# Two transformer blocks on one core: first input projection by feature rows, modulation sums by pairs of feature tiles, side reads moved

## The reference, cut to what matters

```python
mod = c_act @ w_ada[l] + b_ada[l]                  # 1024 -> 3072
shift, scale, gate = jnp.split(mod, 3, axis=-1)
h = rms_norm(x, g_pre[l]) * (1.0 + scale[:, None, :]) + shift[:, None, :]
proj = h @ w_in[l]                                 # 1024 -> 3072: u_a b_a c_a gate_a u_p gate_p, 512 each
y_a = b_a * causal_depthwise_conv(c_a * u_a, w_conv[l]) * jax.nn.silu(gate_a)
y_p = causal_multiscale_pool(u_p, w_pool[l], pool_scale[l]) * jax.nn.silu(gate_p)
y = jnp.concatenate([y_a, y_p], axis=-1) @ w_out[l]
x = x + gate[:, None, :] * rms_norm(y, g_post[l])
```

## Time and profile before

| | |
|---|---|
| median of 3 runs | 1283.83 us (1282.14 to 1292.85) |
| the profiled execution | 1283.65 us, its span 1281.9 us |
| TensorE busy | 1246.6 us (97%), 7756 matmuls |
| VectorE, ScalarE, GpSimd busy | 887.8, 641.3, 171.9 us |
| mean granted TensorE clock | 0.993 of full speed |
| read from memory | 234.92 MB, mean 184 GB/s |

### The profile page before, as it was taken

The page is one execution under the profiler, slowest core; times in us unless marked ns, Lnnn a source line. Parts: engine busy times, 40 slices in busy tenths (PEclk is TensorE's granted clock), DMA queues, the critical chain, the costliest instruction groups (busy, mean ns, idle before and its releaser), DMA issues.

```text
span 1281.9 us, 19570 instructions
## 1 busy us (share of the span) xinstructions
PE 1246.6 (97%) x7756; PEld 1109.8 (87%) x7756; DVE 887.8 (69%) x931; ACT 641.3 (50%) x825; POOL 171.9 (13%) x217
## 2 busy tenths in 40 slices
PE   3899999999999999989999999999999999999998
PEld 2899899888888899978988888888889998988887
DVE  5779666676666767987766667666667787766665
ACT  2445545554444456855544444444446675644442
POOL 8400100088200120000100001000001221200000
PEclk9999899999999999999999999999999999999999
DMA  9897495455556462314555654655554444455551
GB/s 361 262 324 270 158 326 185 145 197 183 186 189 196 121 215 66 132 67 131 187 182 189 196 186 144 227 197 191 182 186 164 148 147 157 151 187 196 196 196 66
DMA packets 166816, 236.88 MB, mean 185 GB/s; under 512 B 5140, under 2 KB 146592, under 8 KB 164704
## 3 DMA queue, kind: packets, MB, share of 16 engines
q1 hardware_dynamic: 165920, 235.09, 54.9%
q0 software_dynamic: 816, 0.89, 0.3%
q10 hardware_dynamic: 16, 0.00, 0.0%
HBM read 234.92 MB, written 1.05 MB: 184 GB/s over the span
## 4 chain that ended last, share of the span: by engine, by line
PE 85%; DVE 6%; DMA 4%; ACT 2%; POOL 1%; issue 1%; DVEq 0%; ACTq 0%; POOLq 0%
PE acc L2185 23%; PE acc L2187 12%; PE acc L2221 5%; PE acc L2222 5%; PE acc L2223 5%; PE acc L2203 4%; PE acc L2204 3%; PE acc L2205 3%; DVE wlo L1349 2%; DMA raw<-in_w_ada_dram 2%; PE acc L2239 2%; PE acc L2593 2%; DMA raw<-in_w_in_dram 2%; PE acc L2241 2%; PE acc L2240 2%; PE acc L2122 2%
## 5 line engine op out<-in xcount | busy, mean ns | idle before, releaser
L1349 DVE TENSOR_TENSOR wlo<-raw,whi 128x2048 fp32r<-128x2048 f32 (+1 forms) x199 | 453.8, 2283 | 199.7 <-ACT whi L745 198.7
L745 ACT ACTIVATE whi<-raw 128x2048 fp32r<-128x2048 f32 (+1 forms) x199 | 378.1, 1904 | 184.3 <-PE acc L2223 113.1
L2185 PE MATMUL acc<-hT,whi 128*128 128x512 f32 x1280 | 320.2, 392 | 0.5 <-ACTq L826 0.5
L2185 PEld LDWEIGHTS acc<-hT,whi 128*128 128x128 f32 x1280 | 232.4, 189 | 43.9 <-issue 0.7
L2187 PEld LDWEIGHTS acc<-hT,wlo 128*128 128x128 f32 x1280 | 174.6, 190 | 12.5
L2187 PE MATMUL acc<-hT,wlo 128*128 128x256 f32 x1280 | 178.5, 282 | 0.0
L2221 PE MATMUL acc<-whi,sT_hi 128*128 128x512 f32 x320 | 125.0, 391 | 0.0
L2222 PE MATMUL acc<-wlo,sT_hi 128*128 128x512 f32 x320 | 125.0, 390 | 0.0
L2223 PE MATMUL acc<-whi,sT_lo 128*128 128x512 f32 x320 | 124.5, 389 | 0.0
L2203 PE MATMUL acc<-whi,hT 128*128 128x256 f32 x416 | 120.2, 289 | 1.1 <-DVE hT L1423 1.1
L2204 PE MATMUL acc<-wlo,hT 128*128 128x256 f32 x416 | 117.6, 283 | 0.0
(11 more groups left out here) (324 smaller groups left out, 1950.6 us busy)
## 6 DMA issues: line engine op xcount, KB each, us to landing
raw<-in_ffn_w_in_dram SPq DMA_DIRECT2D x88, 1024.0 KB, 5.1
raw<-in_ffn_w_out_dram SPq DMA_DIRECT2D x44, 1024.0 KB, 5.0
raw<-in_w_ada_dram SPq DMA_DIRECT2D x24, 1024.0 KB, 5.9
raw<-in_w_in_dram SPq DMA_DIRECT2D x24, 1024.0 KB, 5.9
raw<-in_diff_w_in_dram SPq DMA_DIRECT2D x12, 1024.0 KB, 5.2
raw<-in_nsa_w_in_dram SPq DMA_DIRECT2D x10, 1024.0 KB, 5.3
raw<-in_w_out_dram SPq DMA_DIRECT2D x8, 1024.0 KB, 4.9
raw<-in_nsa_cmp_w_dram SPq DMA_DIRECT2D x4, 1024.0 KB, 5.5
```

Of the source, the lines that this page charges most:

```text
L745: nc.scalar.activation(whi[:, w % SPL, 0:n], raw[:, r % RAW, 0:n], ACT.Copy).then_inc(hi_ready, 1)
L1349: nc.vector.tensor_tensor(wlo[:, w % SPL, 0:n], raw[:, r % RAW, 0:n], whi_f[:, w % SPL, 0:n], ALU.subtract).then_inc(raw_done, 1)
L2185: nc.tensor.matmul(o, hi[:, kt, cs], hT[:, :, kt, :], start=kt == 0, stop=False)
```

## The change

Layer 0 alone, up to its end:

- The shift and scale weights of layer 0 are read in four pairs of feature tiles. A pair is two items of 1 MB (each 4 row tiles by 256 columns of shift and 256 of scale, as two transfers). VectorE sums them in 8 `add_row` of 128 x 512, each waiting for the one before. TensorE sums over partitions (`sum_pair`), VectorE makes shift and gain of the two tiles (`pair_modulation`), ScalarE their features and `hT_hi` (`features`), VectorE `hT_lo` (`features_lo`).
- Half of `w_in` (columns 1536 to 3071) is read as 8 row items, one per feature tile (128 x 1536, 768 KB). TensorE adds each into six PSUM banks, 30 matmuls an item (`row_high`, `row_low`, `row_last`). Four of the banks are cleared with zeros first. The other half stays six column chunks (`cols1`).
- x is loaded first. The turned x is copied out of PSUM before the modulation is known. `b_ada` and `g_pre` are loaded by ScalarE's queue; GpSimd issues its parameter loads after the inverse norms. `keep_clock` shrinks from 5 calls to 1.
- The side items move: none among the rows, then two between column chunks, then one between output chunks.
- ScalarE, VectorE and TensorE have the layer's program written out by hand.

```diff
-    items = [("ada", 0, kt) for kt in range(KD)]
-    side = [("gate", 0, c) for c in range(4)] + [("ada", 1, kt) for kt in range(KD)]
-    for n, c in enumerate(IN1_ORDER):
-        items.append(("w", "in1", 0, c))
-        if n in SIDE_CHUNKS:
-            items.append(side.pop(0))
...
+    items = pair(0) + rows(0) + pair(1) + rows(1, 2) + pair(2) + rows(3, 4) + pair(3) + rows(5, 6, 7)
+    cols = [("w", "in1", 0, c) for c, _ in COLS1]
...
+    items += cols[0:2] + gate[0:2] + cols[2:3] + gate[2:4] + cols[3:4] + ada[0:2] + cols[4:5] + ada[2:4] + cols[5:6]
+    items += ada[4:6] + outs[0:1] + ada[6:7] + outs[1:2] + ada[7:8] + outs[2:4]
```

On ScalarE:

```diff
+            def features(f):
+                act.wait_ge(pair_ready, f + 1)
...
+                for k in range(2):
+                    kt = 2 * f + k
+                    step(nc.scalar.activation(h_pair[:, f % 2, k, :], xT[:, kt, :], ACT.Identity,
+                                              bias=shift1[:, 0, kt:kt + 1], scale=gain1[:, 0, kt:kt + 1]))
+                    nc.scalar.activation(hT_hi[:, kt, :], h_pair[:, f % 2, k, :], ACT.Copy).then_inc(feat_hi, 1)
...
+            split_to(0)
+            features(0)
+            split_to(1)
+            features(1)
+            split_to(2)
+            split_to(3)
+            features(2)
+            split_to(4)
+            split_to(5)
+            features(3)
```

On VectorE:

```diff
+            def add_pair(f):
+                dst = acc_pair[:, f % 2, :, :]
+                for half in range(2):
...
+                    for k in range(4):
+                        ins = add_row(dst, raw[:, r % RAW, k * 512:(k + 1) * 512].rearrange("p (s n) -> p s n", s=2),
+                                      4 * half + k)
+                        if k < 3:
+                            step(ins)
...
+            add_pair(0)
+            row_lo(1)
+            pair_modulation(0)
+            features_lo(0)
+            add_pair(1)
+            row_lo(1)
+            pair_modulation(1)
+            row_lo(1)
+            features_lo(1)
+            add_pair(2)
+            row_lo(1)
+            pair_modulation(2)
+            row_lo(1)
+            features_lo(2)
+            add_pair(3)
+            row_lo(1)
+            pair_modulation(3)
+            features_lo(3)
+            row_lo(2)
...
+                    stream_to(b0 + 4)
+                    modulation(0, 1)
+                    lambda_parts()
+                    pooled_y(0)
+                    stream_to(b0 + 5)
+                    ada_chunks(2)
```

Then `c_a * u_a` and two `y_low`, and:

```diff
+                    stream_to(b0 + 6)
+                    convolve(0)
+                    step(nc.vector.tensor_tensor(v1[:, :, :], v1[:, :, :], pf[:, 12:16, :], ALU.mult))
+                    stream_to(b0 + 7)
```

On TensorE:

```diff
+            sum_pair(0)
+            keep_clock(1)
+            row_high(0, False)
+            row_high(0, True)
+            row_low(0)
+            row_high(1, False)
+            row_high(1, True)
+            sum_pair(1)
+            row_low(1)
```

Rows 2 to 6 follow in the same way, with `sum_pair(2)` behind the first part of row 3 and `sum_pair(3)` behind the second of row 5. Then:

```diff
+            row_last(7)
...
+            cols1(0)
+            pe.wait_ge(proj_ready, 2)
+            pooled_means(0)
+            cols1(1)
+            pe.wait_ge(u_ready, TT)
+            sum_modulation(0, 1)
+            pe.wait_ge(proj_ready, 3)
+            cols1(2)
+            pe.wait_ge(proj_ready, 8)
+            mix_pooled(0)
+            cols1(3)
+            cols1(4)
+            spread_gate(0)
+            cols1(5)
```

More of the change, by code:

```diff
@@ L359, in source @@
         def source(item):
+            if item[0] == "pair":
+                f, half = item[1:]
+                return a["w_ada"][0][half * 512:(half + 1) * 512, 0:2 * D]\
+                    .rearrange("(k p) (s n) -> p k s n", p=P, s=2)[:, :, :, f * CC:(f + 1) * CC]
             if item[0] == "ada":
@@ L365, in source @@
             kind, *at = item[1:]
+            if kind == "row":
+                return a["w_in"][0][at[0] * P:(at[0] + 1) * P, ROW0:ROW0 + ROWN].rearrange("(k p) n -> p k n", p=P)
             if kind == "in1":
@@ L420, in pair_bank, with transfers @@
             return (6 if l == 0 else 2) if c == 0 else 0
+        def transfers(r):
+            return 2 if items[r][0] == "pair" else 1
         def landed_value(r, it=0):
-            return it * (16 * 6 // RAW) + 16 * (r // RAW + 1)
+            return it * (16 * 6 // RAW) + sum(transfers(q) for q in range(r % RAW, r + 1, RAW)) * 16
         block = ctx.enter_context(nc.Block())
@@ L434, in load @@
                 src = source(items[r])
+                if items[r][0] == "pair":
+                    for s in range(2):
+                        sp.dma_start(raw_view(r % RAW, src)[:, :, s, :], src[:, :, s, :]).then_inc(raw_landed[r % RAW], 16)
+                    return
                 sp.dma_start(raw_view(r % RAW, src), src).then_inc(raw_landed[r % RAW], 16)
@@ new lines, in sum_pair, with row_high @@
+            def sum_pair(f):
+                pe.wait_ge(pair_sums, f + 1)
+                for j in range(4):
+                    ins = nc.tensor.matmul(acc[:, 6, 4 * f + j:4 * f + j + 1],
+                                           acc_pair[:, f % 2, j // 2, (j % 2) * P:(j % 2 + 1) * P], ones[:, 0:1],
+                                           start=True, stop=True)
+                ins.then_inc(pair_ps, 1)
+            def row_high(kt, low):
+                w = w_at[("row", kt)]
+                hi = whi[:, w % SPL, 0:ROWN]
+                src = hT_lo if low else hT_hi
+                if low:
+                    pe.wait_ge(feat_ready, kt + 1)
+                else:
+                    pe.wait_ge(feat_hi, kt + 1)
+                    pe.wait_ge(hi_ready, w + 1)
+                for tt in range(TT):
+                    nc.tensor.matmul(acc[:, 4 + tt, :], src[:, kt, tt * P:(tt + 1) * P], hi[:, CW:2 * CW],
+                                     start=kt == 0 and not low, stop=False)
+                for c, b in ROW_GATES:
+                    for ft in range(2):
+                        at = (c - 6) * CC + ft * P
+                        nc.tensor.matmul(acc[:, b, ft * T:(ft + 1) * T], hi[:, at:at + P], src[:, kt, :],
+                                         start=False, stop=False)
@@ new lines, in row_low @@
+            def row_low(kt):
+                w = w_at[("row", kt)]
+                lo = wlo[:, w % SPL, 0:ROWN]
+                chunk_ready(w)
+                for tt in range(TT):
+                    nc.tensor.matmul(acc[:, 4 + tt, :], hT_hi[:, kt, tt * P:(tt + 1) * P], lo[:, CW:2 * CW],
+                                     start=False, stop=False)
+                for c, b in ROW_GATES:
+                    for ft in range(2):
+                        at = (c - 6) * CC + ft * P
+                        ins = nc.tensor.matmul(acc[:, b, ft * T:(ft + 1) * T], lo[:, at:at + P], hT_hi[:, kt, :],
+                                               start=False, stop=False)
+                ins.then_inc(chunk_used, 1)
```

487 lines of the change are left out of this document (318 added, 169 removed).

## The result

The changed kernel takes 1304.82 us (median of 4 runs, 1303.67 to 1305.01), the kernel before beside it 1287.51 (1282.14 to 1292.85); the ratio, which is formed over the runs and is not the quotient of the two medians (1.0134), is 1.0145, 95% interval 1.0113 to 1.0177. So it is slower, by the amount of the forecast, 1303.5. The profiled execution has a span of 1303.1 us; before it had 1281.9.

A forecast was written before the change was run, and what follows sets the result against it. Layer 0 was taken to be bound by loads chained through three slots, no longer by TensorE. Its end moves 16.8 us behind 140.06, plus 3 for clock: 1283.65 + 16.8 + 3 = 1303.5 us, range 1288 to 1316.

The forecast's parts named there:

- Start: Start of layer 0: VectorE begins `add_pair(0)` at 15.0 us, where it began to sum at 6.29 before.
- Row stage: Layer 0's four pairs and rows, followed through VectorE's work and its waits for ScalarE: row 6 done at 70.0 us.
- Links: Column stage: six chained steps of landing, split and low part, 9.65 us each, 57.9 plus 0.5, to 128.4 us.
- Tail: Behind the first output chunk: 17.3 us of VectorE work to 145.7, then TensorE's last chunk pair, 11.2, to 156.9.
- Clock: Row stage: TensorE's low clock after gaps makes VectorE wait for three pairs' sums, 3 us added.
- The third rival: TensorE at half clock through the row stage, 5 us a pair, 15 in all: 1315 us; 14%.
- The first: Loads keep ahead and TensorE runs on from 24 us, layer 0 ending at 128 to 129: 1272 us; 8%.
- The shorter chain: Cheaper adds, shorter links, no clock loss, better ScalarE overlap: layer 0 ends 4 to 10 us later, 1288 to 1294; 18%.

The follow-up runs named there:

- e5: The changed kernel with half of VectorE's adds of layer 0's shift and scale left out, loads unchanged: 1305.13 us, ratio 1.0164.
- e6: The changed kernel with GpSimd's three small loads issued when 10 items are used up, at about 50 us, instead of 16, at 72 us: 1306.0 us.
- e9: The changed kernel with ScalarE copying out the gate row before it splits the second output chunk, not behind it: 1304.99 us, ratio 1.0148.
- e3: The changed kernel with ScalarE splitting rows 2 and 4 ahead of the features of pairs 1 and 2 instead of behind them: 1302.53 us, ratio 1.0147.
- e8: The changed kernel with GpSimd's three small loads issued right behind the inverse norms, at about 9.3 us, not at 72 us: 1305.81 us, ratio 1.0154.
- after: The changed kernel itself, with no further edit, against the kernel before: 1304.82 us, ratio 1.0145.
- e4: The changed kernel with ten more filler matmuls of 128 x 512 in TensorE's row-stage gaps, to keep its clock: 1305.85 us, ratio 1.0172.

## Why the prediction was right, point by point

**Start.** `add_pair(0)` was put at 15.0 and begins at 13.76. The 512-column adds were put at 0.78, from a line through the other sizes. Eight take 14.28 + 5.53 - 13.76 = 6.05 us, of 6.0; the pairs begin at 24.7, 39.6 and 53.7, of 25.6, 40.7 and 55.0.

**Row stage.** Row 6's low part was put at 70.0, without what the clock costs, and ends at 70.15, with it. The start had been 1.2 us early, and pair 3 took longer than its 12.25: VectorE waits 2.86 us up to 64.48 for a sum that TensorE does at a granted clock of 0.66, 1.3 us more than in the profiles where that clock is 1.00. TensorE's start, "about 24", is 23.44. As e5 shows, the sum of VectorE's work was the right number but only half of the reason.

**Links.** Six were put at 57.9 + 0.5 us, and took 62.9, from 70.15 to 133.1. One by one (end of low part to end of low part): 9.45, 12.6, 9.4, 9.4, 10.3, 11.8, where 9.65 was predicted. This is the term that was mis-sized, by 4.5 us; in the other six profiles of this order the six links take 61.6 to 64.5. Three of the deviations:

- Columns 3 to 5 land in 5.0 to 5.1 us, a little less than the 5.3 taken. Column 2 takes 8.2 and the first output chunk 7.6 (121.30 to 128.87, with side items requested 5 and 2 us before it); the prediction's upper bound, with two requests in the queue, was 5.9. I had written off GpSimd's small loads at nothing ("beyond 80 us"); they are issued from 72.43. e6 shows that such loads can cost 2 us, and by the seven profiles they cost column 2's link between nothing and 1.8 us. What makes the rest of it long stays open. The estimate of 4.4 us by the Trainium skill (DMA: Bandwidth & Descriptors, Anatomy of one DMA) was met by no link: the shortest landing among them is 5.0, and the figure is for the software path, while these loads are issued by SP.
- Column 5's low part waits 1 us for VectorE, which is at two side items until 118.94.
- The first link is as predicted here, and was lucky to be. Column 1's load, requested at 70.18, lands 5.0 us later; its split starts at 75.38, just behind ScalarE's copy of `p0` (1.03 us at 74.45), which waits 2.9 us for TensorE's row 7. In the other six profiles this copy comes later, with the half clock in rows 6 and 7, and the link is 11.0 us. The prediction had no such term.

**Tail.** Put at 17.3 from the first output chunk's low part to the third's; it is 133.1 to 150.4, 17.3. The last pair of chunks, put at 11.2, takes 11.0. TensorE's own 24.8 us of work from 136.71 happen to end at the same moment; e9 shows that it is the low parts that count.

**Clock.** 3 us were added for three pairs' sums. The mechanism is there, at one of the three: 1.3 us ahead of pair 3's sum. Half clock does occur, in places that I had not named: 0.50 from 95 to 105 us, behind the 5.6 us wait for the gate, and 0.50 from 135 to 140. So the clock was put 1.7 us too high and the start 1.2 too late, and by luck this hid 2.9 of the 4.5 us by which the links were too short: 16.8 + 3 = 19.8 was predicted for the layer, 21.4 measured. That the time came within 1.4 us of the forecast is more than its terms deserved. Of the page's rule (the Trainium skill, TensorE: Matmul & The Clock Gate, HAM oscillation), that every burst behind a load starts slow, the traces show half: behind gaps of 5.6 and 7.3 us the clock is 0.50, between the rows, with waits for splits of up to 2.5 us, its mean is 0.95, with 0.66 in its lowest 5 us. The third rival, half clock throughout, is out.

**A mark that was wrong.** I said that TensorE would show gaps of 3 to 5 us between column chunks. It has one of 5.6, ahead of the gate's sum at 97.52, and then none until 129.4: it is behind the low parts by up to 8.8 us (column 2: 92.2 and 100.9), through that wait and the half clock after it, and by column 5 by less than 2. The chain of loads still sets the end: TensorE has done its columns 3.7 us before the first output chunk's low part is there.

**The rivals.** The first, TensorE running on from 24 us, is out by the splits 9 to 12 us apart. The shorter chain: its pieces are tested by e5 (adds: 0.5 to 2.1 us at row 6, for three times the saving it named) and e3 (ScalarE's rounds: 3.6, of 3 named), and they would not have been enough with links this long.

## What to carry to other kernels

With n slots, an item waits for the item n before it. Before changing an order, write down for each item which one that is, and whether the load of one can lie beside the split and use of another. Two cheap items in a row between expensive ones make with three slots a closed chain of landing, split and use, 9.3 us and more for each item here, whatever the engines have spare. An earlier start of the busiest engine (13.7 us here) is worth nothing if what feeds it then sets the pace.

Small loads are not free just because nobody waits for them: ask which large one lands beside them. Beside row 5 they cost 2 us (e6); beside column 2 the same bytes could not be told from scatter. One pair of profiles does not price an effect of 1 or 2 us: put every profile with the same order side by side first. And when a gain is booked from one edit, look at what stands at the place to which the work is moved.

## What the runs showed of the hardware that I had not expected

- 1 MB loads out of one queue and in one stretch land in 5.0 to 5.1 us (columns 3 to 5), 6.5 (column 2 in e8), 7.6 (the first output chunk) and 8.2 (column 2 in after, with three small loads of GpSimd beside it, 768 KB together). The same load of column 2, with the same small loads beside it, takes 6.7 to 8.2 us over five profiles; column 4's, 5.1 in after, took 7.5 in e4. What makes them long stays open.
- A half clock in the row stage turns up in one profile ahead of pair 3's sum and in others over rows 6 and 7. It costs 1.3 us in the first place and 1.6 in the second, and ten fillers left the stage's mean clock at 0.95.
- A filler matmul of float32, 128 x 512, is two matmuls in the trace and takes 0.87 us at full clock, where one of the projection's 512-column matmuls takes 0.23.
- Up to row 6, the same order of work in four profiles differs by up to 1.7 us in when it is done, 1.3 of it by the clock; what follows layer 0, some 1133 us, differs by 2.4 us over fourteen kernels.
